# Sandwich macaron block on Trainium2: the two down-projections in seven block products, with weight sums made by accumulating DMAs

## The chip, the cores and the metric

The kernel runs on one core of a Trainium2 chip (TensorE, VectorE, ScalarE, GpSimd and SyncE beside 16 DMA engines). The metric is the device time of one execution in microseconds, the median of several.

## The reference

One layer of a streaming encoder on 512 tokens of width 1024, all fp32: an FFN, a token mixing, an FFN. The part that the change concerns is each FFN's second matrix product, followed by a norm:

```python
def swiglu(h, w_gate, w_up, w_down):
    return (jax.nn.silu(h @ w_gate) * (h @ w_up)) @ w_down      # (512,1024) -> (512,4096) -> (512,1024)

h = rms_norm(x, g_ffn1_pre[l])
x = x + 0.5 * rms_norm(swiglu(h, w_ffn1_gate[l], w_ffn1_up[l], w_ffn1_down[l]), g_ffn1_post[l])
...
x = x + rms_norm(merged @ w_out[l], g_mix_post[l])
h = rms_norm(x, g_ffn2_pre[l])
x = x + 0.5 * rms_norm(swiglu(h, w_ffn2_gate[l], w_ffn2_up[l], w_ffn2_down[l]), g_ffn2_post[l])
```

## The kernel before, in words

Every fp32 product is made of three float32r products: an operand is split into a rounded copy (`_hi`, made by ScalarE with a Copy) and the rest (`_lo`, made by VectorE with a subtraction), and TensorE adds hi·hi, hi·lo and lo·hi in PSUM. So each piece of weights ("unit", 128 partitions by 1024 columns, 512 KB) goes through a load by SP into one of four slots of `w_raw`, a ScalarE copy, a VectorE subtraction, and then TensorE.

Gate and up of both FFNs (`pair`, `blocks`) already work by seven block products instead of eight: the operands are cut in 2x2 blocks, and sums of blocks are multiplied. VectorE makes those sums of weights itself (`sum_t1` to `sum_t4`). Their result goes to `act`, 32 row tiles of 128 FFN rows by 512 tokens.

The down-projection (`down`, `last_down`) is plain: for each of the 32 row tiles f, one unit of `w_down` (row tile f, all 1024 columns) and one slice `a_hi`/`a_lo` of `act` (128 by 512) give 8 output pieces (4 token tiles by 2 column halves, the 8 PSUM banks), three matmuls of 512 columns each: 24 matmuls for a unit, 768 for an FFN. The last four units go token tile by token tile (`last_down`), so that the norm of one tile (`y_spread` on ScalarE, `into_stream` on VectorE) runs beside the next tile's products. After FFN 1 `transposed` and `values_sb` of the mixing stage are put between.

The order of the work is written out by hand on each engine; semaphores join them. `unit_done` counts units that TensorE finished, `w_hi_done` and `w_lo_done` the splits, `raw_full` the loads. `ud` in the code is the number of units before the down-projection. At its start SP waits for `unit_done` = `ud` (the last product of gate and up), because `x_tok` lies where an operand of that product was, and then issues x_tok (4 loads), two tables (FFN 1 only) and the remaining units of `w_down`, each with a wait for its slot.

```python
def step(f, slot, tiles=range(TT), first=False):
    pe.wait_ge(w_lo_done, f + ud + 1)
    pe.wait_ge(a_lo_done, f + NF * fi + 1)
    ...
            mm = row_product(2 * t + dh, a_hi[slot][:, tok(t)], a_lo[slot][:, tok(t)], slot, dh * T, first, False)
```

Of the kernel before, what the change touches and what calls it, by code (L numbers as in the profile page):

```python
# [44 lines left out]

PLACE = {7: 0, 5: 1, 4: 2, 3: 3, 1: 4, 2: 5, 6: 6}
# [23 lines left out]
U_V = U_DOWN1 + NF  # L70
# [5 lines left out]
U_END = U_DOWN2 + NF  # L76


def raw_turn(u):

    return u // SLOTS - (PRODUCTS * NG - SLOTS * NG) // SLOTS * ((u >= U_DOWN1) + (u >= U_DOWN2))
# [98 lines left out]
def build(nc, x, gains, w_gate1, w_up1, w_down1, w_in, w_proj_sb, w_proj_ret, w_out,  # L180
          w_gate2, w_up2, w_down2, const, decay_t, rope_t, x_mid, out):
    with ExitStack() as ctx:
# [46 lines left out]
        act, ea = place("act", [P, NG, 2, T], at=act_at)  # L229
# [24 lines left out]
        a_hi, a_lo, e = [], [], ea  # L254
        for i in range(SLOTS):
            a_hi.append(place(f"a_hi{i}", [P, T], F32R, at=e)[0])
            a_lo.append(place(f"a_lo{i}", [P, T], F32R, at=e + T * 4)[0])
            e += 2 * T * 4

        a21_hi, e = place("a21_hi", [P, KH, HALF], F32R, at=act_at + 6 * T * 4)  # L260
        a21_lo, e = place("a21_lo", [P, KH, HALF], F32R, at=e)
        b22_hi, e = place("b22_hi", [P, UNIT], F32R, at=act_at + 14 * T * 4)
        b22_lo, e = place("b22_lo", [P, UNIT], F32R, at=e)
        g_f, e = place("g_f", [P, 2, D], at=act_at + 22 * T * 4)
        xn_f, e = place("xn_f", [P, 2, D], at=e)
# [9 lines left out]

        xn, en = place("xn", [P, 2, D], at=region)
        g_b, en = place("g_b", [P, 3, D], at=en)
        junk, en = place("junk", [P, D], at=en)

# [32 lines left out]
        assert en == act_at + 6 * T * 4  # L312
# [18 lines left out]
        silu_done, a_done, a_hi_done, a_lo_done = sem("silu_done"), sem("a_done"), sem("a_hi_done"), sem("a_lo_done")  # L331
# [47 lines left out]
        G_TILE = (g_f[:, 0, :], g_b[:, 1, :], g_b[:, 2, :], g_f[:, 0, :], g_f[:, 1, :], g_b[:, 2, :])  # L379

        XN, JUNK = (xn_f, xn, xn_f), (junk_f, junk, junk_f)
# [35 lines left out]
        FIRST, SECOND = slice(0, HALF), slice(HALF, T)  # L417
# [13 lines left out]
        def _(sp_eng):  # L431
# [18 lines left out]
            def ffn_loads(fi, u0, wg, wu, wd, x_src):  # L450
# [34 lines left out]


                sp_eng.wait_ge(t_done, (fi + 1) * N_T)
                for slot in (RAW11, RAW21, RAW12):
                    fetch(slot, rows(wd, slot))
                fetch(RAW22, rows(wd, RAW22), (w_lo_done, ud))  # L490

                sp_eng.wait_ge(unit_done, ud)
                if fi:
                    sp_eng.wait_ge(x_left[0], 32)
                    sp_eng.wait_ge(x_left[1], 32)
                for t in range(TT):
                    sp_eng.dma_start(x_tok[:, t, :], x_src[tok(t), :]).then_inc(x_back, 16)
                if fi == 0:
                    sp_eng.dma_start(decay[:, :, :], decay_t).then_inc(tables_in, 16)
                    sp_eng.dma_start(rope[:, :, :], rope_t).then_inc(tables_in, 16)  # L500
                with sp_eng.Fori(1, NF // SLOTS) as turn:
                    i = turn * SLOTS
                    for j in range(SLOTS):
                        fetch(j, rows(wd, i + j), (w_lo_done, i + ud + j - (SLOTS - 1)))
# [4 lines left out]

            sp_eng.wait_ge(a_lo_done, 12)  # L510
            gain(G_POST1)
            gain(G_PRE_MIX)
            u = U_V
            for c0 in (C_VSB, C_VR):
                for j in range(4):
                    src = w_in[2 * j * P:(2 * j + 2) * P, c0 * P:c0 * P + T].rearrange("(k p) c -> p k c", p=P)
                    load(u, u % SLOTS, src)
                    u += 1
            for t in range(TT):
                sp_eng.wait_ge(x_done, t + 1)  # L520
                sp_eng.dma_start(x_mid[tok(t), :], x_tok[:, t, :]).then_inc(x_spilled, 16)
# [22 lines left out]
            sp_eng.wait_ge(a_lo_done, NF + 12)  # L544
            gain(G_POST2)
# [12 lines left out]
        def _(pe):  # L558
# [145 lines left out]
            def down(fi, u0):  # L704

                ud = u0 + PRODUCTS * NG

                def step(f, slot, tiles=range(TT), first=False):
                    pe.wait_ge(w_lo_done, f + ud + 1)
                    pe.wait_ge(a_lo_done, f + NF * fi + 1)  # L710
                    for t in tiles:
                        if first and t == 1:
                            pe.wait_ge(summed, N_SUMS * (fi + 1))
                        if first and t == 0:
                            pe.wait_ge(a_done, NF * (fi + 1))
                        for dh in range(2):
                            mm = row_product(2 * t + dh, a_hi[slot][:, tok(t)], a_lo[slot][:, tok(t)], slot, dh * T,
                                             first, False)
                    mm.then_inc(unit_done, 1)

                step(0, 0, (2, 3, 1, 0), True)
                with pe.Fori(0, (NF - SLOTS) // SLOTS - 1) as turn:
                    i = turn * SLOTS + 1
                    for j in range(SLOTS):
                        step(i + j, (j + 1) % SLOTS)
                for f in range(NF - LAST - 3, NF - LAST):
                    step(f, f % SLOTS)

            def last_down(fi, u0, t):

                for f in range(NF - LAST, NF):
                    if t == 0:
                        pe.wait_ge(w_lo_done, f + u0 + PRODUCTS * NG + 1)
                        pe.wait_ge(a_lo_done, f + NF * fi + 1)
                    slot = f % SLOTS
                    for dh in range(2):
                        mm = row_product(2 * t + dh, a_hi[slot][:, tok(t)], a_lo[slot][:, tok(t)], slot, dh * T,
                                         False, f == NF - 1)
                    if t == TT - 1:
                        mm.then_inc(unit_done, 1)  # L740
                if t < TT - 1:
                    mm.then_inc(y_ready, 1)
# [12 lines left out]
            down(0, U_UP1)  # L755

            def values_sb(t):

                pe.wait_ge(h_lo_done, TT + t + 1)
                for j in range(4):  # L760
# [7 lines left out]
                    if t == TT - 1:  # L768
                        mm.then_inc(unit_done, 1)
                if t < TT - 1:  # L770
                    mm.then_inc(v_ready, 1)

            last_down(0, U_UP1, 0)
            last_down(0, U_UP1, 1)
            last_down(0, U_UP1, 2)
            transposed(1, 0)
            last_down(0, U_UP1, 3)
            transposed(1, 1)
            values_sb(0)
            transposed(1, 2)  # L780
            values_sb(1)
            transposed(1, 3)
            values_sb(2)
# [182 lines left out]
            down(1, U_UP2)  # L966
            for t in range(TT):
                last_down(1, U_UP2, t)
# [3 lines left out]
        def _(act_eng):  # L972
# [17 lines left out]
            def y_spread(n, t, last_unit):  # L990

                if t < TT - 1:
                    act_eng.wait_ge(y_ready, (TT - 1) * n + t + 1)
                else:
                    act_eng.wait_ge(unit_done, last_unit + 1)
                act_eng.activation(JUNK[n + 1 if n < 2 else n][:, :], bank_pair(t).rearrange("p b c -> p (b c)"), ACT.Square,
# [77 lines left out]
            def first_silu(fi, u0, half):  # L1074
                act_eng.wait_ge(unit_done, u0 + (2, 5)[half])
                act_eng.activation(act[:, 0, :, (FIRST, SECOND)[half]], bank_cols(B_GATE[half]), ACT.Silu
# [22 lines left out]
            def silu(p, sums, second):  # L1099
                act_eng.wait_ge(summed, sums)  # L1100
                act_eng.activation(act[:, p, :, SECOND if second else FIRST], pair_cols(u2_c if second else m1_c),
                                   ACT.Silu).then_inc(silu_done, 1)

            def ffn(fi, u0):
# [3 lines left out]
                def turn_of(p, par, last=False):  # L1108
# [11 lines left out]
                    if last:  # L1120
                        split_u(ud)
                        part(0)
                        split_u(ud + 1)
# [4 lines left out]

                def part(f):

                    if f < 2:
                        act_eng.wait_ge(a_done, NF * fi + 2)
                        act_eng.wait_ge(unit_done, u0 + made(NG - 1, 7))
                    elif f < SLOTS:
                        act_eng.wait_ge(a_done, NF * (fi + 1))
                    else:
                        act_eng.wait_ge(unit_done, f + ud - (SLOTS - 1))
                    act_eng.activation(a_hi[f % SLOTS][:, :], act[:, f // 2, f % 2, :], ACT.Copy).then_inc(a_hi_done, 1)
# [19 lines left out]
                split_u(ud + AHEAD)  # L1158
                part(1)
                split_u(ud + AHEAD + 1)  # L1160
                part(2)
                split_u(ud + AHEAD + 2)
                part(3)
                for f in range(3, SLOTS + 1):
                    split_u(ud + AHEAD + f)
                    part(f + 1)
                with act_eng.Fori(1, (NF - SLOTS) // SLOTS - 1) as i:
                    for j in range(1, SLOTS + 1):
                        v = j + AHEAD
                        split(i * 4 + ud + v, v % SLOTS, i + raw_turn(ud) + v // SLOTS)  # L1170
# [705 lines left out]
```

## Time and profile before

| | |
|---|---|
| median of 3 runs | 1453.03 us (1452.92 to 1453.18) |
| profiled execution, its own time | 1453.62 us |
| its span | 1451.9 us |
| TensorE busy | 1415.8 us (98%) |
| VectorE / ScalarE / GpSimd busy | 890.2 (61%) / 653.9 (45%) / 55.1 us (4%) |
| DMA | 152.40 MB, mean 105 GB/s |
| first down-projection | 346.8 to 523 us |
| second down-projection | 1268.7 to 1444.9 us |

The span is from the first to the last instruction; the execution's own time holds 1.7 us more around it. TensorE's busy time has overlapping records, so its pace is better read from the starts of successive matmuls. All other numbers that matter stand as rows below.

### The profile page before, as it was taken

Reading aid. Unit: us, or ns where it says so; the run is one execution under the profiler, and the core shown is the slowest. Engines: PE = TensorE matmul, PEld = TensorE weight load, DVE = VectorE, ACT = ScalarE, POOL = GpSimd, SP = SyncE. Lnnn points to the kernel's source line nnn. Section 1 sums busy time; section 2 is a strip of 40 time slices with the busy share of each in tenths; the row PEclk is TensorE's granted clock in tenths of the full one; section 3 lists DMA queues with packets and bytes.
Section 4 is the critical chain, followed back from the end, with each engine's and each line's share of the span. In section 5 each row is a group of like instructions: output and inputs, shape, how many; then the busy total and the mean of one; then the engine's idle time right before and its main releaser. Section 6 shows DMA issues by size and latency. Waiting matters only on the chain.

```text
span 1451.9 us, 23228 instructions
## 1 busy us (share of the span) xinstructions
PE 1415.8 (98%) x8840; PEld 1266.5 (87%) x8840; DVE 890.2 (61%) x998; ACT 653.9 (45%) x937; POOL 55.1 (4%) x116
## 2 busy tenths in 40 slices
PE   6999999999999999999989999989999999999997
PEld 6999999999888878767768888889999999988886
DVE  6977788775433364657664343687777877643334
ACT  6544454444322343657763323554445544433222
POOL 0000000000000000333220000000000000000000
PEclk9999999999999999999999999999999999999999
DMA  5323333235322333211113254233233332352221
GB/s 196 103 79 110 116 116 101 79 109 215 118 101 97 120 116 102 76 56 58 45 44 87 87 159 167 85 112 102 83 105 116 116 101 84 104 190 99 101 87 58
DMA packets 131677, 152.40 MB, mean 105 GB/s; under 512 B 4784, under 2 KB 115632, under 8 KB 131504
## 3 DMA queue, kind: packets, MB, share of 16 engines
q1 hardware_dynamic: 130912, 149.97, 31.9%
q10 hardware_dynamic: 720, 1.84, 0.4%
q8 instruction: 28, 0.46, 0.1%
q14 instruction: 17, 0.14, 0.0%
HBM read 145.49 MB, written 6.29 MB: 105 GB/s over the span
## 4 chain that ended last, share of the span: by engine, by line
PE 88%; DVE 6%; ACT 2%; DMA 1%; issue 1%; POOL 1%; SPq 0%; DVEq 0%; ACTq 0%; POOLq 0%
PE ps L615 15%; PE ps L618 14%; PE ps L617 14%; PE ps L588 9%; PE ps L589 9%; PE ps L590 8%; PE ps L581 5%; PE ps L582 5%; PE ps L583 5%; PE ps L878 1%; DVE w_lo L1373 1%; DVE ps L1389 1%; DMA w_raw<-w_ffn_down 1%; DVE x_tok L1392 1%; PE ps L833 1%
## 5 line engine op out<-in xcount | busy, mean ns | idle before, releaser
L1373 DVE TENSOR_TENSOR w_lo<-w_raw,w_hi 128x1024 fp32r<-128x1024 f32 (+1 forms) x132 | 152.9, 1160 | 290.5 <-ACT w_hi L984 289.5
L615 PE MATMUL ps<-s_hi,w_hi 128*128 128x256 f32 x960 | 273.1, 285 | 4.8 <-DVE w_lo L1455 4.8
L617 PE MATMUL ps<-s_lo,w_hi 128*128 128x256 f32 x960 | 272.9, 284 | 0.0
L618 PE MATMUL ps<-s_hi,w_lo 128*128 128x256 f32 x960 | 272.9, 284 | 0.0
L984 ACT ACTIVATE w_hi<-w_raw 128x1024 fp32r<-128x1024 f32 (+1 forms) x132 | 131.5, 1004 | 246.6 <-PE ps L590 222.1
L615 PE MATMUL ps<-a_hi,w_hi 128*128 128x256 f32 x816 | 233.1, 286 | 3.1 <-DVE a_lo L1410 3.0
L617 PE MATMUL ps<-a_lo,w_hi 128*128 128x256 f32 x816 | 232.5, 285 | 0.0
L618 PE MATMUL ps<-a_hi,w_lo 128*128 128x256 f32 x816 | 232.5, 285 | 0.0
L1051 ACT ACTIVATE w_hi<-w_sum 128x1024 fp32r<-128x1024 f32 x120 | 123.9, 1056 | 175.5 <-DVE w_sum L1482 80.4
L588 PE MATMUL ps<-w_hi,a_hi 128*128 128x512 f32 x512 | 199.6, 390 | 1.0 <-DVE a_lo L1566 0.9
L589 PE MATMUL ps<-w_lo,a_hi 128*128 128x512 f32 x512 | 199.2, 389 | 0.0
L590 PE MATMUL ps<-w_hi,a_lo 128*128 128x512 f32 x512 | 199.2, 389 | 0.0
L615 PEld LDWEIGHTS ps<-s_hi,w_hi 128*128 128x128 f32 x960 | 185.6, 193 | 5.1 <-DVE w_lo L1455 5.1
L617 PEld LDWEIGHTS ps<-s_lo,w_hi 128*128 128x128 f32 x960 | 185.6, 193 | 0.0
L618 PEld LDWEIGHTS ps<-s_hi,w_lo 128*128 128x128 f32 x960 | 185.6, 193 | 0.0
L615 PEld LDWEIGHTS ps<-a_hi,w_hi 128*128 128x128 f32 x816 | 158.4, 194 | 3.9 <-issue 3.6
L617 PEld LDWEIGHTS ps<-a_lo,w_hi 128*128 128x128 f32 x816 | 158.4, 194 | 0.0
L618 PEld LDWEIGHTS ps<-a_hi,w_lo 128*128 128x128 f32 x816 | 158.3, 194 | 0.0
L1455 DVE TENSOR_TENSOR w_lo<-w_sum,w_hi 128x1024 fp32r<-128x1024 f32 x120 | 141.2, 1217 | 0.2
L1455 DVE TENSOR_TENSOR w_lo<-w_raw,w_hi 128x1024 fp32r<-128x1024 f32 x90 | 109.9, 1223 | 40.9 <-ACT w_hi L1048 40.8
L581 PE MATMUL ps<-h_hi,w_hi 128*128 128x512 f32 x288 | 118.4, 411 | 0.0
L588 PEld LDWEIGHTS ps<-w_hi,a_hi 128*128 128x128 f32 x512 | 96.1, 188 | 22.0 <-DVE w_lo L1373 1.7
(176 smaller groups left out, 2133.2 us busy)
## 6 DMA issues: line engine op xcount, KB each, us to landing
w_raw<-w_ffn_gate SPq DMA_DIRECT2D x64, 512.0 KB, 5.3
w_raw<-w_ffn_up SPq DMA_DIRECT2D x64, 512.0 KB, 4.8
w_raw<-w_ffn_down SPq DMA_DIRECT2D x64, 512.0 KB, 3.3
w_raw<-w_in SPq DMA_DIRECT2D x44, 512.0 KB, 3.8
x_mid<-x_tok SPq DMA_DIRECT2D x8, 512.0 KB, 5.0
x_tok<-x_mid SPq DMA_DIRECT2D x8, 512.0 KB, 6.0
w_raw<-w_out SPq DMA_DIRECT2D x8, 512.0 KB, 5.7
x_tok<-x SPq DMA_DIRECT2D x6, 512.0 KB, 5.1
```

The source lines that it names most:

```text
L581: pe.matmul(ps[:, bank, out_cols], wh, src_hi, start=first, stop=False)
L582: pe.matmul(ps[:, bank, out_cols], wh, src_lo, start=False, stop=False)
L588: pe.matmul(ps[:, bank, :], s_hi, wh, start=first, stop=False)
L589: pe.matmul(ps[:, bank, :], s_hi, wl, start=False, stop=False)
L590: return pe.matmul(ps[:, bank, :], s_lo, wh, start=False, stop=last)
L615: pe.matmul(o, wh, hi[:, k, :], start=first and f == 0 and k == 0, stop=False, skip_group_check=True)
L617: pe.matmul(o, wh, lo[:, k, :], start=False, stop=False, skip_group_check=True)
L618: mm = pe.matmul(o, wl, hi[:, k, :], start=False, stop=last and k == KH - 1, skip_group_check=True)
L984: act_eng.activation(w_hi[slot][:, 0:cols], w_raw[:, slot, 0:cols], ACT.Copy).then_inc(w_hi_done, 1)
L1051: act_eng.activation(w_hi[slot][:, :], w_sum[slot][:, :], ACT.Copy).then_inc(w_hi_done, 1)
L1373: dve.tensor_tensor(w_lo[slot][:, 0:cols], w_raw[:, slot, 0:cols], w_hi[slot][:, 0:cols].bitcast(F32), ALU.subtract).then_inc(w_lo_done, 1)
L1455: dve.tensor_tensor(w_lo[slot][:, :], whole_w, w_hi[slot][:, :].bitcast(F32), ALU.subtract).then_inc(w_lo_done, 1)
```

## The change

Both down-projections are computed in seven block products. The blocks are: tokens in two halves, the FFN's row tiles in even and odd ones, output columns in two halves. A block of weights is 16 row tiles by 512 columns, eight units of two row tiles each (`DOWN_UNITS`); a product is eight units, an FFN 56. A unit gives 2 row tiles x 2 token tiles x 3 = 12 matmuls of 512 columns, an FFN 672.

Three products (1, 2, 3) take a block of `w_down` as it is, through `w_raw`. The other four (7, 6, 4, 5) take sums of blocks, which are built one from another in `d_sum` (8 units, 4 MB): SP loads a block there, ScalarE changes its sign in place (`negate`), and GpSimd issues DMAs from `w_down` with `accum_op=add` on top of it, two units (1 MB) each. There are 16 accumulating DMAs and 16 plain loads into `d_sum` for an FFN, beside 24 loads into `w_raw` (32 before). The left operands are split in chunks of 128 by 1024 (`chunk_hi`, `chunk_lo`, 28 for an FFN) and their sums made in place in `act` by VectorE (`down_sum`, 16). Partial results are kept and added by `d_m1`, `d_m7`, `d_u2` and finally `last_sum`. Norms of the first two token tiles move in between the chunks of the last products (`first_norms`, `first_outputs`). The loops over row tiles become straight code.

```diff
+DOWN_ORDER = (1, 7, 6, 4, 5, 2, 3)
+DOWN_UNITS = 8
+CHUNKS = 4
+LEFT = 3
...
@@ sync: ffn_loads @@
                 sp_eng.wait_ge(unit_done, ud)
+                for q in range(DOWN_UNITS):
+                    sum_load((0, 1), q)
+                for q in range(SLOTS, DOWN_UNITS):
+                    fetch(q % SLOTS, down_block((0, 0), q), (w_lo_done, ud + q - SLOTS + 1))
+
                 if fi:
                     sp_eng.wait_ge(x_left[0], 32)
                     sp_eng.wait_ge(x_left[1], 32)
                 for t in range(TT):
                     sp_eng.dma_start(x_tok[:, t, :], x_src[tok(t), :]).then_inc(x_back, 16)
-                if fi == 0:
-                    sp_eng.dma_start(decay[:, :, :], decay_t).then_inc(tables_in, 16)
-                    sp_eng.dma_start(rope[:, :, :], rope_t).then_inc(tables_in, 16)
-                with sp_eng.Fori(1, NF // SLOTS) as turn:
...
+                for q in range(SLOTS):
+                    fetch(q, down_block((1, 0), q), (w_lo_done, ud + SLOTS + q + 1))
+
+                for q in range(DOWN_UNITS):
+                    sp_eng.wait_ge(w_lo_done, ud + DOWN_ORDER.index(4) * DOWN_UNITS + q + 1)
+                    sum_load((0, 0), q)
...
@@ tensor @@
+            def down_unit(fi, ud, u, tiles=(0, 1), last=False):
...
+                for g in range(2):
+                    cols = slice(g * T, (g + 1) * T)
+                    for tile in tiles:
...
+                        pe.matmul(o, sh, wh[:, cols], start=first and g == 0, stop=False, skip_group_check=True)
+                        pe.matmul(o, sh, wl[:, cols], start=False, stop=False, skip_group_check=True)
+                        mm = pe.matmul(o, sl, wh[:, cols], start=False, stop=last and g == 1, skip_group_check=True)
@@ scalar: ffn @@
+                for n in range(PRODUCTS * CHUNKS):
+                    if n:
+                        chunk_hi(fi, ud, n)
+                        unit_hi(fi, ud, 2 * n)
+                    unit_hi(fi, ud, 2 * n + 1)
+
+                    for first, begin in ((0, 0), (8, 9), (16, 14)):
+                        if begin <= n < begin + CHUNKS:
+                            for q in (2 * (n - begin), 2 * (n - begin) + 1):
+                                negate(fi, ud, first, q)
...
+            def unit_hi(fi, ud, u):
+                ph, q = divmod(u, DOWN_UNITS)
+                m = DOWN_ORDER[ph]
+                act_eng.wait_ge(unit_done, ud + u - (SLOTS - 1))
+                if m in (1, 2, 3):
...
+                else:
+                    act_eng.wait_ge(r_full[q // 2], 64 * fi + 16 * ph)
+                    src = d_sum[:, q, :]
+                act_eng.activation(w_hi[u % SLOTS][:, :], src, ACT.Copy).then_inc(w_hi_done, 1)
+
+            def negate(fi, ud, first, q):
+                if first == 8:
+                    act_eng.wait_ge(w_lo_done, ud + DOWN_ORDER.index(6) * DOWN_UNITS + q + 1)
+                else:
+                    act_eng.wait_ge(r_load[q], 32 * fi + (16 if first == 0 else 32))
+                act_eng.activation(d_sum[:, q, :], d_sum[:, q, :], ACT.Copy, scale=-1.0).then_inc(r_neg, 1)
@@ vector: ffn @@
+                for n in range(PRODUCTS * CHUNKS):
+                    if n:
+                        chunk_lo(fi, n)
+                        unit_lo(ud, 2 * n)
+                    unit_lo(ud, 2 * n + 1)
+                    if n < 4 * CHUNKS:
+                        down_sum(fi, n)
...
@@ gpsimd @@
+            def weight_sums(fi, ud, wd):
+                for step, (j, d) in enumerate(((1, 1), (0, 0), (1, 0), (0, 1))):
+                    for i in range(DOWN_UNITS // 2):
+                        if step == 1:
+                            pool.wait_ge(w_lo_done, ud + DOWN_ORDER.index(7) * DOWN_UNITS + 2 * i + 2)
+                        else:
+                            pool.wait_ge(r_neg, 24 * fi + DOWN_UNITS * (0, 0, 1, 2)[step] + 2 * i + 2)
+                        src = wd.rearrange("(g j p) c -> p g j c", j=2, p=P)[:, 4 * i:4 * i + 4, j, d * T:(d + 1) * T]
+                        dst = d_sum[:, 2 * i:2 * i + 2, :].rearrange("p q (g c) -> p (q g) c", g=2)
+                        pool.dma_start(dst, src, accum_op=ALU.add).then_inc(r_full[i], 16)
```

SyncE's queue at the start of the first down-projection. Before:

```order
L462 DMA w_raw<-w_ffn_down 128x1024 [waits w_lo_done]
L497 DMA x_tok<-x 128x1024 [waits unit_done]
L497 DMA x_tok<-x 128x1024 x3
L499 DMA decay<-decay_t 128x2048
L500 DMA rope<-rope_t 128x1024
```

The same place in the change:

```order
L500 DMA w_raw<-w_ffn_down 128x2x512 [waits w_lo_done]
L531 DMA d_sum<-w_ffn_down 128x2x512 [waits unit_done]
L531 DMA d_sum<-w_ffn_down 128x2x512 x7
L500 DMA w_raw<-w_ffn_down 128x2x512 [waits w_lo_done] x4
L549 DMA x_tok<-x 128x1024 x4
L500 DMA w_raw<-w_ffn_down 128x2x512 [waits w_lo_done] x4
L531 DMA d_sum<-w_ffn_down 128x2x512 [waits w_lo_done] x8
```

Eight loads into `d_sum` stand ahead of the fifth unit of the first product, x_tok behind the eighth, and the tables have gone to the next stage.

ScalarE's program around the same moment, from the table load that follows the last Silu on. Before (each `w_hi` has its own raw slot, `a_hi` is 512 wide):

```order
L1157 ACT_TABLE_LOAD
L984 ACTIVATE w_hi_65<-w_raw 128x1024 [waits unit_done,raw_full2]
L1138 ACTIVATE a_hi_103<-act 128x512 [waits unit_done,a_done]
L984 ACTIVATE w_hi_68<-w_raw 128x1024 [waits unit_done,raw_full3]
L1138 ACTIVATE a_hi_105<-act 128x512 [waits a_done]
L984 ACTIVATE w_hi_59<-w_raw 128x1024 [waits unit_done,raw_full0]
```

In the change:

```order
L1221 ACT_TABLE_LOAD
L1262 ACTIVATE w_hi_62<-w_raw 128x1024 [waits raw_full1,unit_done]
L1269 ACTIVATE d_sum<-d_sum 128x1024 [waits r_load0]
L1269 ACTIVATE d_sum<-d_sum 128x1024 [waits r_load1]
L1249 ACTIVATE l_hi_104<-act 128x1024 [waits a_done,unit_done]
L1262 ACTIVATE w_hi_65<-w_raw 128x1024 [waits raw_full2,unit_done]
L1262 ACTIVATE w_hi_68<-w_raw 128x1024 [waits raw_full3,unit_done]
L1269 ACTIVATE d_sum<-d_sum 128x1024 [waits r_load2]
```

Two sign changes, each with a wait for a load, now stand ahead of the splits of units 2 and 3 (`w_hi_65`, `w_hi_68`) and of the second chunk.

## Rows read from the trace of the kernel before

**Rows 1.** The page: busy time, then the chain that ended last.
```profile
PE 1415.8 (98%) x8840; PEld 1266.5 (87%) x8840; DVE 890.2 (61%) x998; ACT 653.9 (45%) x937; POOL 55.1 (4%) x116
...
PE 88%; DVE 6%; ACT 2%; DMA 1%; issue 1%; POOL 1%; SPq 0%; DVEq 0%; ACTq 0%; POOLq 0%
```

**Rows 2.** Stretches (from:to, length; busy and instructions by engine; clock, DMA share, GB/s).
```profile
350.00:360.00 10.00, 10.00 (x45) 8.26 (x45) 1.49 (x2) 0.00 (x0) 0.00 (x0) 1.00 1.00 397
...
396.00:432.00 36.00, 36.00 (x161) 29.80 (x160) 12.71 (x14) 11.06 (x14) 0.00 (x0) 1.00 0.25 90
...
529.00:537.00 8.00, 7.20 (x36) 5.79 (x36) 6.21 (x6) 2.35 (x4) 0.00 (x0) 1.00 0.93 321
```

**Rows 3.** Timeline of TensorE inside the first down-projection (start, length, instruction).
```profile
396.31 0.39 PE L588 MATMUL ps<-w_hi,a_hi 128*128 128x512 f32 x1
396.54 0.39 PE L589 MATMUL ps<-w_lo,a_hi 128*128 128x512 f32 x1
396.77 0.39 PE L590 MATMUL ps<-w_hi,a_lo 128*128 128x512 f32 x1
396.99 0.39 PE L588 MATMUL ps<-w_hi,a_hi 128*128 128x512 f32 x1
```

**Rows 4.** What TensorE waited for, 340 to 580 us.
```profile
PE ps L588 <- DVE w_lo L1373: 0.8, 1, 0.8
PE ps L588 <- DVE h_lo L1410: 0.8, 1, 0.8
```

**Rows 5.** Timeline of ScalarE at the start of the first down-projection.
```profile
346.83 1.06 ACT L984 ACTIVATE w_hi<-w_raw 128x1024 fp32r<-128x1024 f32 x1
347.79 0.61 ACT L1138 ACTIVATE a_hi<-act 128x512 fp32r<-128x512 f32 x1
...
360.53 1.06 ACT L984 ACTIVATE w_hi<-w_raw 128x1024 fp32r<-128x1024 f32 x1 [10.65 <-DMA w_raw<-w_ffn_down]
```

**Rows 6.** Timeline of VectorE, the same place.
```profile
349.66 1.22 DVE L1373 TENSOR_TENSOR w_lo<-w_raw,w_hi 128x1024 fp32r<-128x1024 f32 x1
350.80 0.69 DVE L1597 TENSOR_TENSOR a_lo<-act,a_hi 128x512 fp32r<-128x512 f32 x1
```

**Rows 7.** SyncE's issues, 335 to 400 us.
```profile
347.03 1.75 SPq L497 DMA_DIRECT2D x_tok<-x  x4
```

**Rows 8.** Tile x_tok, 340 to 380 us: its four loads' time to landing.
```profile
DMA to landing us min/median/max: 3.3/5.1/7.1
```

**Rows 9.** DMA issues of the page: each, KB, us to landing.
```profile
out<-x_tok SPq DMA_DIRECT2D x3, 512.0 KB, 2.6
```

**Rows 10.** Chain of waits behind the first down-projection (start, length, what).
```profile
505.55 0.23 PE ps L589
505.78 0.24 PE ps L590
...
506.04 1.12 ACT junk L996 x2
...
507.19 0.30 ACT std L999
...
507.81 1.30 DVE ps L1389
...
509.14 1.24 DVE x_tok L1392
...
510.40 1.16 ACT junk L1008 x2
...
512.17 1.28 DVE xn L1402
```

**Rows 11.** The chain's end, behind the second down-projection.
```profile
1444.65 0.24 PE ps L590
...
1448.78 0.69 DVE x_tok L1392
```

More of the change, by code:

```diff
@@ L713, in step, with down @@
+            def down(fi, u0, between):
+                ud = u0 + PRODUCTS * NG
+                for n in range(PRODUCTS * CHUNKS):
+                    m = DOWN_ORDER[n // CHUNKS]
+                    if n % CHUNKS == 0:
+                        if m == 7:
                             pe.wait_ge(summed, N_SUMS * (fi + 1))
[L714 removed]
                             pe.wait_ge(a_done, NF * (fi + 1))
[L716 to L718 removed]
@@ L719, in step @@
[L719 to L742, printed above, removed]
+                        elif m == 4:
+                            pe.wait_ge(d_copied, 2 * fi + 2)
+                        elif m == 5:
+                            pe.wait_ge(d_summed, 4 * fi + 2)
+                        elif m == 2:
+                            pe.wait_ge(d_copied, 2 * fi + 1)
+                        elif m == 3:
+                            pe.wait_ge(d_summed, 4 * fi + 4)
@@ L754, in _, with first_norms, values_sb @@
             up_rest(0, U_UP1)
-            down(0, U_UP1)
-            def values_sb(t):
+            def first_norms(n):
+                if n in (25, 26):
+                    transposed(1, n - 25)
+            down(0, U_UP1, first_norms)
+            def values_sb(t, between=None):
                 pe.wait_ge(h_lo_done, TT + t + 1)
@@ L769, in values_sb @@
                         mm.then_inc(unit_done, 1)
+                    if j == 1 and between is not None:
+                        transposed(1, between)
                 if t < TT - 1:
                     mm.then_inc(v_ready, 1)
[L773 to L778, printed above, removed]
             values_sb(0)
[L780 to L783, printed above, removed]
+            values_sb(1, 2)
+            values_sb(2, 3)
             values_sb(3)
@@ L965, in _ @@
             up_rest(1, U_UP2)
-            down(1, U_UP2)
-            for t in range(TT):
-                last_down(1, U_UP2, t)
+            down(1, U_UP2, lambda n: None)
         @block.scalar
@@ L1120, in turn_of @@
                     if last:
-                        split_u(ud)
-                        part(0)
-                        split_u(ud + 1)
+                        chunk_hi(fi, ud, 0)
+                        unit_hi(fi, ud, 0)
                     else:
@@ L1157, in ffn @@
                 act_eng.preload_act_table_set("sqrt_and_others")
[L1158 to L1170, printed above, removed]
-                        act_eng.wait_ge(unit_done, i * SLOTS + ud + j + 1 - (SLOTS - 1))
-                        act_eng.activation(a_hi[(j + 1) % SLOTS][:, :], act[:, i * 2 + (j + 1) // 2, (j + 1) % 2, :], ACT.Copy
-                                           ).then_inc(a_hi_done, 1)
@@ new lines, in chunk_lo, with unit_lo @@
+            def chunk_lo(fi, n):
+                ph, c = divmod(n, CHUNKS)
+                dve.wait_ge(l_hi_done, PRODUCTS * CHUNKS * fi + n + 1)
+                dve.tensor_tensor(l_lo[n % LEFT][:, :, :], left_of(DOWN_ORDER[ph], c),
+                                  l_hi[n % LEFT][:, :, :].bitcast(F32), ALU.subtract).then_inc(l_lo_done, 1)
+            def unit_lo(ud, u):
+                ph, q = divmod(u, DOWN_UNITS)
+                src = w_raw[:, q % SLOTS, :] if DOWN_ORDER[ph] in (1, 2, 3) else d_sum[:, q, :]
+                dve.wait_ge(w_hi_done, ud + u + 1)
+                dve.tensor_tensor(w_lo[u % SLOTS][:, :], src, w_hi[u % SLOTS][:, :].bitcast(F32), ALU.subtract
+                                  ).then_inc(w_lo_done, 1)
```

335 lines of the change are left out of this document (216 added, 119 removed).

## The prediction

> **What bounds the kernel now.** I read the page first: TensorE is busy 98% of the span and 88% of the chain that ended last lies on it [rows 1]. So a change pays only by what it takes from TensorE's stream or from a wait of that stream. Next the stretches: inside the first down-projection TensorE is busy 36.00 of 36 us at full clock, VectorE 12.71, ScalarE 11.06, and the DMA engines have a share of 0.25 at 90 GB/s [rows 2]. The reader is to see three idle resources beside a full one. The pace of TensorE is read from starts, not lengths: 396.31, 396.54, 396.77, 396.99, that is 0.227 us for a matmul of 512 columns, though each record is 0.39 long [rows 3]. TensorE's waits from 340 to 580 us are some tenths each, the longest two 0.8 us [rows 4]: nothing to win there. The time to come is therefore one sum: matmuls saved, minus stalls made.
>
> All sums below are against the profiled execution (span 1451.9, own time 1453.62). That is 0.6 us above the median of 1453.03; I apply the difference to the median. 0.2%, 2.9 us, is about what a measurement of this kernel can tell from no change.
>
> **Matmuls.** 768 become 672 for each FFN, all of 128x512. 96 x 0.227 = 21.8 us less for each FFN, 43.6 in all. A unit now takes 12 x 0.227 = 2.72 us, a chunk of two units 5.44, a product of eight units 21.8. TensorE stands at the full clock in these rows, and I see nothing that would lower it.
>
> **VectorE and ScalarE.** A subtraction of 128x1024 starts 1.14 us ahead of the next instruction (349.66 to 350.80) [rows 6], a copy of that shape 0.96 us (346.83 to 347.79) [rows 5]. In a chunk VectorE has one chunk_lo, two unit_lo and, up to chunk 15, one down_sum: 4 x 1.14 = 4.6 of 5.44 us. ScalarE has one chunk_hi, two unit_hi and in twelve chunks two sign changes: 5 x 0.96 = 4.8. Both fit. The single additions of partial results (about 1.2 us each, four on VectorE, two copies on ScalarE) and the norms moved between the last chunks push a few chunks over 5.44 (on VectorE 3.4 + 2.7 for chunk 22, 3.4 + 4.2 for chunk 23), some 3 us together, against splits that run three units (8 us) ahead. I cost them at nothing; without that cover they cost those 3 us.
>
> **Start of each down-projection.** Time here counts from the end of gate and up (346.9). SP issues the eight loads to d_sum at that moment, one per 0.45 us as it does with x_tok [rows 7]. The first of x_tok's landed 3.3 us after its issue [rows 8]; so r_load0 is there at 3.4, r_load1 one transfer (512 KB at 397 GB/s, 1.3 us) later, 4.8. ScalarE's sign changes wait for them and end at 5.8; chunk_hi and unit_hi of unit 2 follow (7.7), VectorE's unit_lo makes it 8.9. TensorE would want unit 2 at 5.4: 3.5 us lost. Unit 4 is worse. Its raw load is ninth behind the sum loads: 9 x 0.524 MB at 397 GB/s is 11.9, plus 2 to landing and two splits of 2.2: 16. Queued behind ScalarE's fourth sign change it is no later. But from 7 us on GpSimd's first accumulating DMA shares the engines. If each queue gets half, the 2.7 MB that are left of the nine loads take 13.6 us instead of 6.8, and unit 4 starts at about 22.5 against 10.9. So 5 to 12 us are lost at the start (the 3.5 is inside it). Before, the same place had a fetch that landed after 10.65 us of ScalarE idling [rows 5] and TensorE waited hardly at all, since four units covered 21.8 us, not 10.9. I take 11.
>
> **The weight sums, the term that decides.** The trace has no accumulating DMA. Before the last of them (the sum for units 38 and 39 of 56) lands, the DMA engines have to carry, in plain bytes, 16 loads to d_sum (8.4 MB), 4 + 4 raw units (4.2) and x_tok (2.1): 14.7 MB, 37 us at 397 GB/s [rows 2]. The 16 accumulating ones are 16.8 MB. Bounds of their price: at best a byte costs what a plain load's does, 42 us in all (factor 1). At worst nothing overlaps, each 512 KB read out of SBUF as a store is (2.6 us [rows 9]) and then written as a load is (3.3 us [rows 8]): 11.8 us for 1 MB, 189 us in all (factor 4.5). Nearest to what it does is one load and one store's reading in one: the destination must be read as well as the source. Stores beside loads shared the engines at 321 GB/s with a share of 0.93 [rows 2], so a read out of SBUF has a load's price. I take factor 2, 84.6 us.
>
> The Trainium skill (Collectives: The Full Stack, The bandwidth ceiling: the fold count and why AG ≠ RS ≠ AR) says that an add inside a DMA engine costs no cycles of its own but two source reads on the same read ring, half the rate of a copy. It speaks against this change; by it the factor is 2 or just under (1.93), and no row of this trace shows it either way. By its other half alone, an add that is free, the sum would be that of factor 1.
>
> With factor 2 the last sum lands at 37 + 84.6 + about 3 to the first landing + some 3 in which the queues have nothing issued (each accumulating DMA waits for a sign change or for the split of the old sum) = 128; two splits later, at 130, TensorE may start unit 38. Its own pace would bring it there at 38 x 2.72 + 11 = 114.4. So another 15 us are lost; I take 14, since some of the DMAs' pauses fall into the first stall. In the rate of a single step: a sum of 1 MB is needed each 5.44 us, and factor 2 takes 5.3 without anything else on the queues, and the second block load (4.2 MB) comes on top.
>
> **Edges.** Behind FFN 1, norms of tiles 0 and 1 and their transposes are now inside the products, but tiles 2 and 3 end together: square, root, two multiplications, square, root and norm are 7 us in a row before a tile can be transposed [rows 10] and VectorE does tiles 2 and 3 one behind the other. Cover is values_sb(0) and half of values_sb(1), 36 matmuls, 8.2 us. With last_sum (0.7) and the splits of U_V in front I get 10 to 11: 1.5 us lost (bounds 0 to 4, where before lost 0.8 [rows 4]). At the kernel's end the last matmul starts at 1444.65 and the last addition at 1448.78 [rows 11]; now tile 2's last product ends only 2.7 us before tile 3's, last_sum (0.7) stands ahead, and two normed multiplications of tile 2 (1.30 + 1.24 [rows 10]) come first: 1.8 us later.
>
> **Sum.** For each FFN -21.8 + 11 + 14 = +3.2, twice +6.4; edges +3.3; together +9.7. 1453 + 10 = **1463 us**.
>
> **The rivals.**
> (a) *Accumulation as cheap as a load.* Then 37 + 42 + 6 = 85 us, long before 106, and only the start is lost. -21.8 + 11 = -10.8, twice -21.6, +3.3: 1435. With a start of 5 us only, 1423. For it: the add could be hidden in a read side that is faster than the write side, which the rows cannot tell apart. Against: the doubled reading. The sides part at the factor where a stall of 9 us is left: 37 + 42.3f + 6 + 2 = 114.4 + 9, f = 1.86. Faster by over 0.2% is anything below about 1.8. This is the case that ends on the other side; 0.38 with its neighbours from 1.0 to 1.8.
> (b) *Much slower accumulation*, by the engines or by GpSimd, which has to write each DMA's many small descriptions itself and waits in order. Factor 2.5: 37 + 105.8 + 8 = 151, 36 us of stall, +25 for each FFN, 1506. Factor 3: 1548. 0.14.
> (c) *The sums hidden or not, the start decides.* If the queues do not share by halves but the accumulating DMA gets two thirds of the time, units 4 to 7 come 3 us later still and the sums earlier: within 3 us of the forecast; it is inside its range.
> (d) *The change doesn't do what it says*: the count of matmuls is fixed by the code, so only if TensorE's pace with two output banks in turn, not eight, were slower. 0.24 us instead of 0.227 would be +9 for each FFN. The last steps before 506 already go between two banks and keep 0.23 to 0.24 with their neighbours [rows 10]. 0.02.
>
> **How the numbers follow.** Forecast, factor 1.9 to 2.4: 0.40, its own range 1457 (-21.8 + 11 + 11 for each FFN) to 1499 (32 us of stall instead). Rival (a) 0.38, from 1425 to 1450; (b) 0.14; (d) 0.02; what lies between forecast and (a), 0.06: no difference. So faster 0.38, same 0.06, slower 0.56. The range holds the forecast's own and most of (a), and of (b) what lies below factor 2.5: 1430 to 1506, leaving about 0.05 below and 0.14 above.
>
> **What would show it.** In the profile after: 0.227 us between matmuls, units 2 and 4 late by a wait on w_lo behind d_sum or w_raw loads; 1 MB accumulating DMAs that land 5 to 8 us after issue in a free queue; a DMA share near 1.0 from the start of each down-projection for about 130 us; ScalarE's unit_hi waiting for d_sum loads in products 4 and 5. Wrong, if accumulating DMAs land in under 5 us beside other traffic and TensorE has no wait behind unit 8 (then rival a), or if GpSimd's queue takes longer than 5.4 us to issue one (then b).

## The result, and the profile after

| | before | change |
|---|---|---|
| median | 1453.07 us (1452.92 to 1453.18, 4 runs) | 1469.84 us (1467.58 to 1472.69, 4 runs) |
| span of the profiled execution | 1451.9 us | 1465.8 us |

The ratio is 1.0121 (95% interval 1.0106 to 1.0137): slower by 1.2%. The profiled execution is the fastest of the four, so it shows 13.9 us of the 16.8. All executions in this document are in the same, fast state of the chip.

The page of the change, the lines that answer to [rows 1], and its software queue and DMA issues (out<-in, engine, count, KB each, us to landing):

```profile
PE 1388.4 (95%) x8648; PEld 1238.6 (85%) x8648; DVE 1018.5 (69%) x1084; ACT 767.5 (52%) x1029; POOL 96.3 (7%) x148
...
q0 software_dynamic: 16896, 33.56, 12.5%
...
PE 72%; DMA 11%; DVE 7%; ACT 5%; issue 3%; POOL 1%; SPq 1%; ACTq 0%; DVEq 0%; POOLq 0%
...
d_sum<-w_ffn_down POOLq DMA_DIRECT2D x32, 1024.0 KB, 14.0
...
d_sum<-w_ffn_down SPq DMA_DIRECT2D x32, 512.0 KB, 9.1
```

TensorE lost 27 us of busy time as intended, but its share of the last chain fell from 88 to 72%, and DMA rose from 1 to 11%. What TensorE waited for in the whole span (us, times, longest), against [rows 4]:

```profile
PE ps L775 <- DVE w_lo L1718: 38.1, 12, 7.5
...
PE ps L648 <- DVE h_lo L1509: 3.0, 1, 3.0
...
PE ps L663 <- DVE xn_m L1501: 1.0, 1, 1.0
```

L775 is the first matmul of a piece in the new down-projection, L1718 the subtraction that ends a unit's split. The named releaser is only the last link: before the copies that stand in front of it (L1262), ScalarE had sat idle 65.8 us for DMAs to `d_sum` and 26.1 us for `w_raw`. The single waits, by TensorE's timeline, are 4.26 us before unit 2 and 6.05 before unit 4 of FFN 1 (4.18 and 7.48 in FFN 2), then between 440 and 480 us 1.42, 3.98, 0.69, 0.24 and 1.29 (FFN 2: 1.70, 4.22, 2.63), for the sums of products 4 and 5.

Stretches of the first down-projection, as in [rows 2] (last three columns: clock, DMA share, GB/s):

```profile
354.00:356.00 2.00, 0.00 (x0) 0.00 (x0) 1.72 (x2) 2.00 (x3) 1.05 (x1) 0.92 1.05 396
356.00:358.00 2.00, 1.21 (x3) 1.05 (x4) 2.00 (x3) 2.00 (x4) 0.00 (x0) 0.50 1.11 378
358.00:360.00 2.00, 2.00 (x6) 1.52 (x6) 1.90 (x2) 0.98 (x2) 1.29 (x1) 0.50 0.98 255
...
404.00:420.00 16.00, 16.00 (x72) 13.28 (x71) 14.80 (x14) 13.89 (x16) 2.56 (x2) 1.00 1.13 207
```

Two things can be read from these rows. From 404 to 420 only accumulating DMAs ran (the queue table of that stretch has q0 alone, 3.31 MB in 16 us), the engines full, and moved 207 GB/s where plain loads moved 397 [rows 2]: factor 1.92. And behind TensorE's wait the granted clock stands at 0.50, the 1.2 GHz level. The timeline there shows it in the pace, 0.43 us from start to start against the 0.227 of [rows 3]:

```profile
356.79 0.77 PE L775 MATMUL ps<-w_hi,l_hi 128*128 128x512 f32 x1 [4.26 <-DVE w_lo L1718]
...
357.78 0.63 PE L777 MATMUL ps<-w_hi,l_lo 128*128 128x512 f32 x1
358.21 0.63 PE L775 MATMUL ps<-w_hi,l_hi 128*128 128x512 f32 x1
358.63 0.63 PE L776 MATMUL ps<-w_lo,l_hi 128*128 128x512 f32 x1
```

Such a stretch, of 3 to 6 us, stands behind each of the six waits of 3.98 to 7.48 us, and behind one shorter wait, the 2.63 us before unit 38 in FFN 2. There it begins four matmuls later:

```profile
1406.09 0.47 PE L775 MATMUL ps<-w_hi,l_hi 128*128 128x512 f32 x1 [2.63 <-DVE w_lo L1718]
...
1407.61 0.63 PE L777 MATMUL ps<-w_hi,l_lo 128*128 128x512 f32 x1
1408.04 0.63 PE L775 MATMUL ps<-w_hi,l_hi 128*128 128x512 f32 x1
```

The waits up to 1.70 us have none behind them. Each matmul of a slow stretch takes 0.2 us more. The seven stretches hold 7 to 13 such matmuls each and cost 1.6 to 2.7 us each, about 16 us together.

The account of TensorE's time, in the profiled executions: matmuls -43.6; waits in the down-projections +38.1, less 1.9 that were there before; half clock +16; waits in the values stage behind FFN 1 4.0 against 0.8, +3.2; from the last matmul's start to the end 9.2 us against 7.2, +2.0. Together +13.8; measured +13.9. The fit is closer than it deserves. TensorE is 6.8 us late where the mixing stage first waits (610.94 against 604.15) and only 4.2 us late at the start of FFN 2's down-projection (1274.17 against 1269.92, where the table of the time before has 1268.7), and nothing that the change did explains those 2.6 us.

The time can be read more simply from the start of unit 38, the first that needs the last sum of weights. Counted from the first matmul of the down-projection it starts 131.1 us later in FFN 1 (477.95) and 131.9 in FFN 2 (1406.09). Without any loss it would be 38 x 2.72 = 103.4.

### The profile page after: what moved, and what is told of

Same layout as the page of the kernel before. It is cut to its first block, busy times and chain, and to the rows that moved or that the text cites. A ratio compares the mean times of both kernels' runs of the same rounds, so it can differ in the third digit from the quotient of the medians.

```text
span 1465.8 us, 22642 instructions
## 1 busy us (share of the span) xinstructions
PE 1388.4 (95%) x8648; PEld 1238.6 (85%) x8648; DVE 1018.5 (69%) x1084; ACT 767.5 (52%) x1029; POOL 96.3 (7%) x148
## 4 chain that ended last, share of the span: by engine, by line
PE 72%; DMA 11%; DVE 7%; ACT 5%; issue 3%; POOL 1%; SPq 1%; ACTq 0%; DVEq 0%; POOLq 0%
PE ps L675 14%; PE ps L677 14%; PE ps L678 14%; DMA d_sum<-w_ffn_down 8%; PE ps L641 5%; PE ps L643 5%; PE ps L642 5%; DMA w_raw<-w_ffn_down 3%; PE ps L775 2%; PE ps L776 2%; PE ps L777 2%; ACT d_sum L1269 2%; PE ps L950 1%; ACT w_hi L1262 1%; PE ps L648 1%
## 5 line engine op out<-in xcount | busy, mean ns | idle before, releaser
L775 PE MATMUL ps<-w_hi,l_hi 128*128 128x512 f32 x448 | 182.8, 408 | 38.2 <-DVE w_lo L1718 38.1
L776 PE MATMUL ps<-w_lo,l_hi 128*128 128x512 f32 x448 | 180.8, 404 | 0.0
L777 PE MATMUL ps<-w_hi,l_lo 128*128 128x512 f32 x448 | 180.2, 402 | 0.0
L775 PEld LDWEIGHTS ps<-w_hi,l_hi 128*128 128x128 f32 x448 | 88.1, 197 | 61.9 <-issue 43.3
L1472 DVE TENSOR_TENSOR w_lo<-w_raw,w_hi 128x1024 fp32r<-128x1024 f32 (+1 forms) x68 | 74.6, 1100 | 90.5 <-ACT w_hi L1054 89.8
L643 PE MATMUL ps<-h_hi,w_lo 128*128 128x512 f32 x288 | 112.4, 390 | 0.0
```

The costliest lines, as they stand in the source:

```text
L643: return pe.matmul(ps[:, bank, out_cols], wl, src_hi, start=False, stop=last)
L775: pe.matmul(o, sh, wh[:, cols], start=first and g == 0, stop=False, skip_group_check=True)
L776: pe.matmul(o, sh, wl[:, cols], start=False, stop=False, skip_group_check=True)
L777: mm = pe.matmul(o, sl, wh[:, cols], start=False, stop=last and g == 1, skip_group_check=True)
L1472: dve.tensor_tensor(w_lo[slot][:, 0:cols], w_raw[:, slot, 0:cols], w_hi[slot][:, 0:cols].bitcast(F32), ALU.subtract).then_inc(w_lo_done, 1)
```

## The experiments

Each was timed beside runs of the kernel before on the same chip (its median there is in brackets). "The change" had 1469.84.

**Is it the adding?** `e_plain`:

```diff
-                        pool.dma_start(dst, src, accum_op=ALU.add).then_inc(r_full[i], 16)
+                        pool.dma_start(dst, src).then_inc(r_full[i], 16)
```

> Edit: the change with GpSimd's 32 DMAs as plain copies (the adding is left out, so the sums of weights are wrong; bytes, queue, waits and all else stay). Theory A (an accumulating byte costs the DMA engines two): 1 MB at about 400 GB/s instead of 207, no TensorE wait behind unit 8 of either down-projection, the first stall shorter too: 1443 to 1452 us against the change's 1470. Rival B (the price is that of GpSimd's queue and its descriptors): nothing moves, 1467 to 1472.

Measured 1442.94 us (1451.51), ratio 0.9938 (0.9921 to 0.9954). The queue is the same, as are the bytes that land; the adding, and with it the reading of what it adds to, is left out. DMA issues and TensorE's waits of e_plain:

```profile
d_sum<-w_ffn_down POOLq DMA_DIRECT2D x32, 1024.0 KB, 7.8
d_sum<-w_ffn_down SPq DMA_DIRECT2D x32, 512.0 KB, 6.2
```

```profile
PE ps L775 <- DVE w_lo L1718: 20.5, 5, 6.1
```

A DMA lands 7.8 us after its issue instead of 14.0, and what is left of TensorE's waits is the start (4.13 and 5.85 us in FFN 1). So the price is that of adding, for the part behind unit 8: its waits fell from 7.6 to 0.3 us in FFN 1. Whether it is the second reading that takes the time or the adding itself, no run here separates. The start is hardly touched. Unit 4 starts 22.9 us after the first matmul of the stage instead of 24.3, so adding costs 1.4 us there. The plain copies still share the engines with SP's loads, so what the sharing costs is not shown by this run. (GpSimd's time per issue fell too, from 1.29 to 0.76 us; `e_small` below shows that this was not what counted.)

**Is it the order at the start?** `e_rawfirst`:

```diff
-                for q in range(DOWN_UNITS):
-                    sum_load((0, 1), q)
-                for q in range(SLOTS, DOWN_UNITS):
-                    fetch(q % SLOTS, down_block((0, 0), q), (w_lo_done, ud + q - SLOTS + 1))
+                for q in range(SLOTS):
+                    sum_load((0, 1), 2 * q)
+                    sum_load((0, 1), 2 * q + 1)
+                    fetch(q, down_block((0, 0), SLOTS + q), (w_lo_done, ud + q + 1))
```

> Edit: SP deals the four raw fetches of units 4 to 7 between the eight d_sum loads instead of behind them. If the first stall is a matter of order (unit 4's fetch ninth in the queue), the wait before unit 4 (6.0 and 7.5 us) and the slow clock behind it (about 3 us each) go: 1450 to 1458. If the DMA engines' total load sets the time, the stall only moves to the sums behind it: 1466 to 1472.

Measured 1471.11 us (1451.51), ratio 1.0134 (1.0117 to 1.0151). TensorE's waits of e_rawfirst by timeline, FFN 1:

```profile
356.26 0.77 PE L775 MATMUL ps<-w_hi,l_hi 128*128 128x512 f32 x1 [4.12 <-DVE w_lo L1718]
...
372.80 0.47 PE L775 MATMUL ps<-w_hi,l_hi 128*128 128x512 f32 x1 [3.12 <-DVE w_lo L1718]
...
385.09 0.80 PE L775 MATMUL ps<-w_hi,l_hi 128*128 128x512 f32 x1 [9.30 <-DVE w_lo L1718]
```

The 6 us before unit 4 are gone, and waits of 3.1 us before unit 6 and 9.3 before unit 7 have come instead. This does not separate bytes from order cleanly, because the edit has a flaw of its own: SP's fetches wait for splits, and the last two d_sum loads now stand behind such a wait (ScalarE's sign changes idle 15.1 us for their loads instead of 7.2). It does show that moving these four transfers in a full queue only moved the wait.

**An earlier start.** `e_early` keeps the bytes and uses that `d_sum` lies on operands that are free before the last product ends. It moves two things at once: the eight `d_sum` loads go earlier, and the four loads of `x_tok` that the diff takes out stand again behind the eight loads of the second block:

```diff
+                sp_eng.wait_ge(unit_done, ud - 5)
+                for q in range(4):
+                    sum_load((0, 1), q)
                 fetch(RAW22, down_block((0, 0), RAW22), (w_lo_done, ud))
-
-                sp_eng.wait_ge(unit_done, ud)
-                for q in range(DOWN_UNITS):
+                sp_eng.wait_ge(unit_done, ud - 2)
+                for q in range(4, DOWN_UNITS):
                     sum_load((0, 1), q)
...
-                if fi:
-                    sp_eng.wait_ge(x_left[0], 32)
-                    sp_eng.wait_ge(x_left[1], 32)
-                for t in range(TT):
-                    sp_eng.dma_start(x_tok[:, t, :], x_src[tok(t), :]).then_inc(x_back, 16)
-
```

> Edit: the eight d_sum loads are issued as soon as the operands below them are done (after five and two units before the end of gate and up) instead of at the end, and x_tok's loads go behind the second block load. Same bytes, earlier start. If the start costs what the trace of the change shows (22 us idle in both, about 12 us of slow clock), those 34 us go: 1434 to 1445, below the kernel before. If the doubled reading alone bounds the stage, the sums behind still hold it up: 1450 to 1460.

Measured 1444.45 us (1451.51), ratio 0.9956 (0.9939 to 0.9973): 25 us below the change, and below the kernel before. TensorE's waits of e_early:

```profile
PE ps L777 <- DVE w_lo L1720: 23.1, 11, 4.3
```

At the start 0.81 us is left; the rest stands between 430 and 465 us, where the sums are late: 1.67, 3.79, 2.24 and 2.51. The last three are each followed by about 3 us at the half clock.

**Is it the clock?** `e_warm` keeps TensorE busy through its two first waits; no load and no split is moved in the program:

```diff
+                    if n in (1, 2):
+                        pe.wait_ge(a_done, NF * (fi + 1))
+                        pe.wait_ge(ident_in, 16)
+                        for i in range((30, 75)[n - 1]):
+                            pe.transpose(ps[:, 3, tok(i % 4)], c(IDENT), c(IDENT))
```

> Edit: the change with 30 transposes of the identity into a free bank ahead of unit 2 and 75 ahead of unit 4, about as long as TensorE's waits there; no load or split moves. Theory C (part of the loss is TensorE's clock, granted at half for some 6 us behind each long wait): no half clock behind unit 2, units 2 to 7 end 3 to 6 us earlier in each down-projection: 1459 to 1465. If the clock behind the waits costs nothing because the sums are later anyway: 1468 to 1474.

Measured 1471.24 us (1451.51), ratio 1.0133 (1.0111 to 1.0156). The same two stretches, first of the change, then of e_warm:

```profile
356.00:362.00 6.00, 5.21 (x12) 4.13 (x13) 4.14 (x4) 2.98 (x4) 1.29 (x1) 0.50 1.06 297
371.00:377.00 6.00, 5.77 (x15) 4.60 (x16) 2.59 (x4) 4.07 (x5) 0.83 (x1) 0.57 1.08 317
```

```profile
356.00:362.00 6.00, 4.22 (x19) 3.51 (x20) 5.13 (x5) 3.98 (x5) 1.33 (x2) 1.00 1.07 332
371.00:377.00 6.00, 5.90 (x30) 4.60 (x29) 3.25 (x3) 4.73 (x5) 1.28 (x1) 1.00 1.09 298
```

The half clock is gone there and the time is the same. Unit 2 even started 0.9 us later in its stage, and TensorE then waited for the next splits instead: unit 8's is made at 383.1 us in e_warm and at 382.7 in the change, and unit 8 starts at 384.5 and 384.9. (In FFN 2 a stretch of 3 us at the half clock stayed, behind a wait of 1.88 us before unit 4.) So of the 16 us of half clock in the account, the two stretches at the start of FFN 1 cost nothing by themselves, and the unchanged time says the same of those in FFN 2; the loads set the time behind them. An account of an engine's time is not a list of what each cause costs.

**Both causes away.** `e_floor` is `e_early` with the plain copies of `e_plain`.

> Edit: the early start of e_early and the plain copies of e_plain in one kernel (the adding is left out, so the sums of weights are wrong). If start and doubled bytes are all that the change loses beside its edges, TensorE has no wait above 1 us in either down-projection, and the time is the kernel before less 43.6 us of matmuls plus some 4 us of edges: 1409 to 1418. If something else costs too (other splits too slow for 5.44 us a chunk, straight code), 1425 or more.

Measured 1417.7 us (1451.85), ratio 0.9754 (0.9732 to 0.9776). Waits of e_floor, 340 to 560 us:

```profile
PE ps L650 <- DVE h_lo L1511: 3.0, 1, 3.0
PE ps L777 <- DVE w_lo L1720: 1.3, 2, 0.8
PE ps L665 <- DVE xn_m L1503: 1.0, 1, 1.0
```

That is 34 us below the kernel before, where 43.6 of matmuls less some 5 of edges would give 38. Start and adding are thus all but 4 us of what the change loses. What the 4 are is not shown. The dense VectorE and ScalarE cost no wait above 0.8 us in the first down-projection; the second has one of 1.06.

**Fewer accumulated bytes.** `e_t1` is `e_early` with product 5's sums on VectorE, in chunks 14 to 17 (its own sums of left operands, `down_sum`, end with chunk 15):

```diff
+                    if SUB_AT <= n < SUB_AT + CHUNKS:
+                        for q in (2 * (n - SUB_AT), 2 * (n - SUB_AT) + 1):
+                            dve.wait_ge(r_load[q], 32 * fi + 32)
+                            dve.wait_ge(raw_full[q % SLOTS], (raw_turn(ud) + 2 + q // SLOTS) * 16 + 16)
+                            dve.tensor_tensor(d_sum[:, q, :], d_sum[:, q, :], w_raw[:, q % SLOTS, :],
+                                              ALU.subtract).then_inc(r_sub, 1)
...
-                for step, (j, d) in enumerate(((1, 1), (0, 0), (1, 0), (0, 1))):
+                for step, (j, d) in enumerate(((1, 1), (0, 0), (1, 0))):
```

> Edit: e_early, and product 5's sums of weights made by VectorE (its block loaded plainly into d_sum, the other through w_raw, one subtraction per unit, 8 for an FFN) in place of 4 accumulating DMAs and 8 sign changes. The engines carry 4.2 MB of 12.6 doubled ones less each time. If the doubled bytes are what holds up units 32 to 40 in e_early (23 us idle in both), that goes: 1415 to 1427. If VectorE then is the bound (6.9 of 5.44 us in chunks 14 and 15), 1428 to 1440.

Measured 1426.52 us (1451.85), ratio 0.9821 (0.9805 to 0.9838). Its waits:

```profile
PE ps L783 <- DVE w_lo L1735: 10.2, 9, 1.8
```

`e_t1only` has this edit without the earlier start.

> Edit: the change itself with product 5's sums made by VectorE as in e_t1, the start untouched. If the two losses are separate, this takes away what the change loses behind unit 8 (16 us idle and some 6 us of slow clock) and leaves the start: 1446 to 1452. If the start alone set the time, 1466 or more.

Measured 1454.42 us (1451.85), ratio 1.0016 (1.0006 to 1.0026): 15 below the change, 2 us above what I expected. Its waits are 28.5 us; the starts are as in the change (4.17 and 5.22 us in FFN 1), the part behind unit 8 has 4.0 instead of 7.6 and no half clock. The two losses are separate: e_early takes away 25.4 us, e_t1only 15.4, and e_t1, which has both edits, 43.3.

**Smaller accumulating DMAs.** `e_small`: one unit (512 KB) and one semaphore each, 64 in place of 32.

```diff
-                    for i in range(DOWN_UNITS // 2):
+                    for q in range(DOWN_UNITS):
...
-                        pool.dma_start(dst, src, accum_op=ALU.add).then_inc(r_full[i], 16)
+                        pool.dma_start(dst, src, accum_op=ALU.add).then_inc(r_full[q], 16)
```

> Edit: the change with accumulating DMAs of one unit each (512 KB, 64 instead of 32), each with its own semaphore. Theory A: same bytes, so within 4 us of the change, if anything earlier since half sums land sooner: 1463 to 1471. Rival B (the price is in GpSimd's issuing, 1.28 us a DMA): twice as many issues, 1475 or more.

Measured 1458.53 us (1451.85), ratio 1.0043 (1.0026 to 1.006). That is 11 us below the change and below my expectation. Rival B falls: GpSimd's issues took 78.0 us instead of 41.3 and it got faster. In the timeline the starts are worse (13.3 us of waits in FFN 1 against 10.3), but behind unit 8 FFN 1's waits are 1.14, 0.86 and 2.06, where the change had 7.6 with one of 3.98: the late ones are short, and no half clock follows them. Where the time comes from is seen in the DMA share before the last sum, first of the change, then of e_small:

```profile
460.00:466.00 6.00, 5.31 (x21) 4.03 (x20) 2.39 (x3) 3.49 (x4) 0.00 (x0) 0.88 1.12 231
466.00:472.00 6.00, 5.75 (x26) 4.46 (x25) 4.76 (x5) 4.32 (x5) 1.30 (x1) 1.00 0.65 104
472.00:478.00 6.00, 4.71 (x22) 3.59 (x20) 2.48 (x3) 2.51 (x3) 0.00 (x0) 1.00 0.52 95
```

```profile
460.00:466.00 6.00, 4.61 (x19) 3.52 (x20) 2.81 (x4) 3.90 (x4) 1.61 (x2) 1.00 1.10 274
466.00:472.00 6.00, 3.94 (x18) 2.95 (x17) 3.42 (x3) 3.07 (x3) 0.80 (x1) 1.00 1.13 209
472.00:478.00 6.00, 6.00 (x28) 4.83 (x27) 4.54 (x5) 4.14 (x5) 0.00 (x0) 1.00 0.17 31
```

In the change the engines are full up to 466 us and then half empty. GpSimd issues the last accumulating DMA only at 466.91, because it waits for a sign change that stands in ScalarE's program behind two copies, and these wait for the sum before. It then lands alone in 8.5 us. With halves the same chain moves in smaller steps, the engines stay full to 472, and unit 38 starts 127.8 and 127.2 us after the stage's first matmul instead of 131.1 and 131.9. So the last sum is late by bytes and, at the end, by this chain. The half clock behind the 3.98 us is not shown to count, since TensorE waited again at unit 38; the stretch behind unit 38 in FFN 2, 1.6 us, is gone in e_small.

The two that followed from it, `e_earlysmall` (e_early with these DMAs) and `e_best` (e_t1 with them):

> Edit: e_early with the accumulating DMAs of one unit each. In e_small that took 10 us of waits and two stretches of half clock from the part behind unit 8, though the engines carried the same bytes. With the start already mended the same should be had here: e_early's 23 us of waits down by 8 to 12, and its slow stretches behind the 3.8 us waits gone: 1430 to 1437. If the bytes alone bound it: 1442 or more.

> Edit: e_t1 (early start, product 5's sums on VectorE) with the accumulating DMAs of one unit each, as in e_small. e_t1 still waits 10 us in all for single sums, none long enough to be followed by the half clock. If those waits are for the second half of a 1 MB DMA, most go: 1419 to 1424. If they are for VectorE or for the first half, it stays at 1425 to 1428.

e_earlysmall: 1439.94 us (1450.93), ratio 0.9926 (0.9911 to 0.9941), 4 to 5 us better than e_early, less than expected. e_best: 1426.85 us (1450.93), ratio 0.9825 (0.9808 to 0.9841), no better than e_t1. Waits of the two, in that order:

```profile
PE ps L777 <- DVE w_lo L1720: 20.7, 16, 2.2
```

```profile
PE ps L783 <- DVE w_lo L1735: 10.0, 11, 2.0
```

e_earlysmall waits in more and shorter pieces, 20.7 us against 23.1, and has two stretches at the half clock in its down-projections where e_early has five. In e_t1, where the longest wait is 1.8 us, the smaller DMAs change nothing; one of e_best's waits, of 2.02 us, even has 3 us of half clock behind it. The best version is thus e_t1: 1.8% below the kernel before and 43 us below the change.

## Why the prediction was right, and where its steps were not

Forecast 1463, range 1430 to 1506, slower with 0.56; measured 1469.84, inside the range and on the side that was held likelier. The range was wide enough to hold most of the rival that ends on the other side. By its steps:

- **Matmuls**: right. 672 at 0.227 where the clock is full; e_floor bears out the gain.
- **VectorE and ScalarE at nothing**: right; e_floor, which has the same work on both, has no wait above 0.8 us in the first down-projection and 1.1 in the second.
- **Start, 11 us an FFN**: the mechanism was right, the term too small. The wait before unit 2 was forecast at 3.5 and measured at 4.26, and unit 4 was to start at about 22.5 us and started at 24.3. But the term stops at unit 4. Units 4 to 7 then took 13.7 us instead of 10.9, and 13.0 in e_warm, where the clock was full, because their splits were late too. Unit 8 started 16.3 us late in FFN 1 and 16.6 in FFN 2. The forecast gave each queue half of the engines; from 360 to 366 us GpSimd's queue had 72% and SP's 38 (the shares add up to more than 100):

```profile
q0 software_dynamic: 394, 0.81, 72.2%
q1 hardware_dynamic: 393, 0.75, 38.0%
```

- **The weight sums, the term that decides**: the factor was right and its cause fits. 397 / 207 is 1.92; e_plain, with rows of the same size on both queues, gives 395 / 207. By the rule of the Trainium skill (Collectives: The Full Stack, The bandwidth ceiling: the fold count and why AG ≠ RS ≠ AR) the add costs a second source read and no more, 1.93 there: the trace agrees in the factor, and no run shows the second read by itself. The forecast had unit 38 start at 130 us; it started at 131.1 and 131.9. The loss between units 8 and 38 was 11.4 and 12.0 us instead of 14, for TensorE came later to the same sums. Some of the lateness at the end is not bytes but the chain through ScalarE that e_small shows; the forecast has it only as "some 3" us of empty queues.
- **Clock, "I see nothing that would lower it"**: this was wrong. The sum itself had stalls of several us in it, and TensorE stood at the half clock behind seven of the waits. By the traces it hardly touched the total. All but one of these stretches lie ahead of unit 38, which waited for the last sum in both FFNs anyway; e_warm shows it for the starts, and for the later ones it is argued from that wait. The one behind unit 38 in FFN 2 cost 1.6 us that the forecast lacks.
- **Edges, +3.3**: +5.2 measured (values stage 3.2, end 2.0). The wait that was forecast there, of the transposes for the norm, was 1.0 us; a larger one for h_lo of the tile behind it (3.0) was not forecast.
- **Rivals**: (a), accumulation as cheap as a load, was put at 1435; e_plain, which makes it true, has 1442.94. Most of the 8 us lie in the start, where unit 8 is 14.3 us late in both FFNs instead of 11. (b) and (d) did not come. The premise of (c), two thirds of the engines for the accumulating DMA, is what the queue shares above show, and the result stayed inside the range, as (c) said; what the sharing costs was not tried.
- **Luck**: some. In the profiled execution FFN 1 with its edge cost 6.8 us (forecast 4.7), FFN 2 7.7 (forecast 3.2) and the end 2.0 (forecast 1.8), 16.5 in all against 9.7. That the execution is only 13.9 us slower is owed to the 2.6 us that came back ahead of FFN 2's down-projection for no reason that is known.

## What to carry to other kernels

Before a compute engine's work is moved to accumulating DMAs, count their bytes twice and set them against the deadline of the last sum, not against the span; here that turned 44 us of fewer matmuls into 17 us more, and one block sum of four given back to VectorE was worth 18 us. Ask of every load at a stage's border when its buffer is really free: issuing eight loads once the operands beneath were done, not the whole stage, and moving `x_tok` behind them was worth 25 us together. Look also at the order in which one engine serves such a chain: near its end the queues stood half empty while a sign change waited its turn. And price a stall of TensorE of a few us with a slow stretch that may stand behind it, but only where nothing else is late anyway.

## What the runs showed of the hardware that I had not expected

- Accumulating DMAs of 1 MB from GpSimd's queue held all 16 engines at 207 GB/s, to the end of a 16 us stretch, with VectorE busy 14.8 of 16 us beside them. Plain copies on the same queue, beside SP's loads, moved 395 GB/s (e_plain, 360 to 376 us).
- TensorE's half clock stood behind all waits of 3.34 to 11.45 us in the down-projections of the runs, for 2.5 to 6 us of work. Among shorter ones the length alone did not decide: one of 3.12 us (e_rawfirst, before unit 6) had none behind it, one of 1.87 us (e_warm, before unit 30) had 3 us, and the wait of 2.96 us for h_lo had some 5 us behind it in e_plain and none in the change. In FFN 1 of e_warm, 105 transposes in the two waits kept the full clock.
- GpSimd was busy 1.29 us for each accumulating DMA of 1 MB (41.3 us for 32), 1.22 for one of 512 KB (78.0 for 64) and 0.76 for a plain one of 1 MB (24.2 for 32).
